# One table set for logarithm and exponential in a two-block transformer kernel

## The chip, the cores and the metric

The kernel runs on one core of a Trainium2 chip. The metric is device time in microseconds (us) of one execution; the time before is the median of three runs. Below, PE is TensorE (matrix products), DVE is VectorE, ACT is ScalarE, POOL is GpSimd and SP is SyncE, which issues nearly all DMAs.

## The reference

An input of 512 tokens by 1024 features passes through a first block of two layers and a second block of two layers, in float32.

```
first block, per layer:
  h = rmsnorm(x, g_pre_mix);  z = h @ w_in
  mLSTM mixer (silu, log_sigmoid gates, exp) and sliding-window attention (softmax)
  x = x + rmsnorm(y @ w_out, g_post_mix)
  h = rmsnorm(x, g_pre_ffn)
  u = causal_dwconv(h @ w_up);  y = (silu(gate) * val) @ w_down
  x = x + rmsnorm(y, g_post_ffn)
second block, per layer, on 512 tokens and (layer 0) 256 context tokens:
  h = rmsnorm(x) modulated by silu(c) @ w_mod;  z = h @ w_in
  pooling, neighborhood attention (softmax), retention (exp decays, silu gate)
  x = x + mod * (y @ w_out);  x = x + mod * conv_ffn(modulated rmsnorm(x))
out = rmsnorm(x, final_g)
```

Every rmsnorm needs x * (mean(x*x) + eps)^(-1/2). The kernel computes the factor on ACT as exp(-0.5 * ln(mean + eps)).

## The kernel before, in words

Features lie on the 128 partitions, tokens on the free axis. A matrix product is done tile by tile (128 output features): each float32 operand is split into a high and a low part, and PE adds three products, high*high, low*high and high*low (`pe_chunk`, line 1011). Per tile, the weights are loaded by SP into `STAGE`, ACT copies them rounded into `WH` (`split_high`, line 850), DVE subtracts to get `WL` (`split_low`, line 856). The same is done with the activations, `HH` and `HL`. The ring of weight buffers has six slots, but four in the third and the fourth of the five streams named below.

The program is a chain of five streams of such products with a mixer (attention and recurrence) between each two. In a stream, every change from one product to the next passes through a *head*, which has its instructions written out in a fixed order on each engine:

- The squares of the last product's output are summed, PE forms their mean (lines 331 and 334), and then runs 24 filler products whose result nobody reads (`idle`, line 257).
- `Rstd.act` (lines 378 to 382) runs on ACT: Ln of the mean (line 380), then, after its own semaphore, Exp (line 382).
- DVE waits for the factor. In `GainHead` it scales y (line 597), adds it to x (line 660), ACT writes the high part (line 638) and a square (line 352), DVE the low part (line 647). In `NormHead` DVE scales x (line 727), ACT writes the high part (line 707), DVE the low part (line 738). PE waits for the low part of each of the eight chunks and multiplies the first three tiles chunk by chunk.
- A `GainHead` has a second `Rstd`, called late: PE is already multiplying unscaled rows, and the factor is multiplied in where DVE takes a tile out of PSUM (line 970, or `to_z1`).
- The one `NormHead` with a gain runs a first `Rstd`, then squares x again on ACT (line 701) with PE summing (line 749), 24 more fillers, then a second `Rstd`.
- `MixHead` (446 to 449) and `RetentionHead` (509 to 531) follow the mixers and have a Ln and an Exp of their own.

ACT can evaluate a function only if the table set loaded in it holds that function. `preload_act_table_set(name)` puts a load of a named set into the program; where a function is not in the current set, the build puts one in, and the profile shows it as ACT_TABLE_LOAD at the line of the instruction that needs it. So line 382 has an ACT_TABLE_LOAD ahead of its Exp although the code asks for none.

Of the kernel before, what the change touches and what calls it, by code (L numbers as in the profile page):

```python
# [46 lines left out]
V2_LP = V2_CB + 44  # L47
V2_N = V2_LP + 6


C_ID, C_BLK, C_RR = 0, 128, 256
C_KE = 384
# [9 lines left out]
def ranges(tokens):  # L62

    return [(0, SEQ)] + ([(SEQ, CTX)] if tokens == TOK else [])
# [17 lines left out]
def by_bank(ap, tokens):  # L82

    return ap if tokens == SEQ else ap.rearrange("p (b s) -> p b s", b=2)
# [20 lines left out]
def later(n):  # L105

    return not isinstance(n, int) or n > 0
# [6 lines left out]
def build(nc, a, out):  # L114
    ctx = ExitStack()
    with ctx:
# [4 lines left out]
        def sb(name, shape, dt=F32, offset=None):  # L121
            size = 4 * int(np.prod(shape[1:]))
            if offset is None:
                offset = used[0]
                used[0] += (size + 31) // 32 * 32
            return nc.alloc_sbuf_tensor_at(name, shape, dt, offset=offset)
# [28 lines left out]
        U = [sb(f"U{s}", [P, SEQ], offset=o_tmp + (2 + 2 * s) * TOK * 4) for s in range(2)]  # L155
# [152 lines left out]
        class Squares:  # L308
# [6 lines left out]
            def act(self, act, c, src, tokens):  # L315
                if c > 1:
                    act.wait_ge(sq_added.sem, sq_added.at(self.added + max(1, c - 2)))
                act.activation(SQ[c % 2][:, 0:tokens], src, ACT.Square).then_inc(sq_done.sem, 1)  # L318
# [174 lines left out]
        class RetentionHead(Head):  # L493
# [13 lines left out]
            def act(self, act):  # L507
                n = self.tokens
                act.activation(Z[:, RG:RG + 3, 0:n], Z[:, RG:RG + 3, 0:n], ACT.Silu).then_inc(gate_done.sem, 1)  # L509
                act.preload_act_table_set("natural_log")  # L510
                self.copied(act, 0)
                self.copied(act, 1)
                self.run.split_high(act, 0)
                for c in range(3):
                    act.wait_ge(centred.sem, centred.at(c + 1))
                    act.activation(GROUP[c][:, 0:n], Z[:, RQ + c, 0:n], ACT.Square).then_inc(group_sq.sem, 1)
                for c in range(2, 5):
                    self.copied(act, c)
                self.run.split_high(act, 1)
                for c in range(3):  # L520
                    act.wait_ge(var_ps.sem, var_ps.at(c + 1))
                    act.activation(GROUP[c][:, 0:n], PS[VAR_PS[c]][:, 0:n], ACT.Ln,
                                   bias=EPSC[:, 0:1]).then_inc(group_ln.sem, 1)
                self.run.split_high(act, 2)
                for c in range(3):
                    act.wait_ge(group_ln.sem, group_ln.at(c + 1))
                    act.activation(GROUP[c][:, 0:n], GROUP[c][:, 0:n], ACT.Exp, scale=-0.5).then_inc(group_rstd.sem, 1)  # L527
                for c in range(5, DC):
                    act.wait_ge(group_out.sem, group_out.at(2 * (c - 4)))
                    self.copied(act, c)  # L530
                for u in range(3, self.run.ring):
                    self.run.split_high(act, u)
# [67 lines left out]
        class GainHead(Head):  # L600
# [21 lines left out]
            def act(self, act):  # L622
                if self.gain:
                    self.before.wait_mean(act)
                    self.first.act(act)
                    act.preload_act_table_set("natural_log")
                else:
                    act.preload_act_table_set("natural_log")
                    act.wait_ge(vec_in.sem, vec_in.at(16))
                    act.wait_ge(filled.sem, filled.at(5))  # L630
                for c in range(DC):
                    if self.gain:
                        act.wait_ge(added.sem, added.at(self.y0 + c + 1))
                    else:
                        if c in self.SPLIT_AT:
                            self.run.split_high(act, self.SPLIT_AT[c])
                        act.wait_ge(x_in[c].sem, x_in[c].at(16))
                    act.activation(self.hi[:, c, :], X[:, c, 0:SEQ], ACT.Identity, scale=self.scale(c),
                                   bias=ZERO[:, 0:1]).then_inc(h_hi.sem, 1)
                    self.squares.act(act, c)  # L640
                if not self.gain:
                    for u in range(4, self.run.ring):
                        self.run.split_high(act, u)
# [29 lines left out]
        class NormHead(Head):  # L673
# [16 lines left out]
            def act(self, act):  # L690
                n = self.tokens
                self.before.wait_mean(act)
                if self.gain:
                    self.first.act(act)
                    act.preload_act_table_set("natural_log")
                    act.wait_ge(ctx_in.sem, ctx_in.at(16))
                    for c in range(DC):
                        act.wait_ge(added.sem, added.at(self.y0 + c + 1))
                        if c > 1:
                            act.wait_ge(xsq_summed.sem, xsq_summed.at(self.x0 + c - 1))  # L700
                        act.activation(SQ[c % 2][:, 0:n], X[:, c, 0:n], ACT.Square).then_inc(xsq_done.sem, 1)
                    act.wait_ge(xsq_summed.sem, xsq_summed.at(self.x0 + DC))
                self.norm.act(act)
                for c in range(DC):
                    act.wait_ge(t_done.sem, t_done.at(self.t0 + c + 1))
                    for st, (t0, tn) in enumerate(ranges(n)):
                        ins = act.activation(self.hi[:, c, t0:t0 + tn], T1[c % 2][:, t0:t0 + tn],
                                             ACT.Identity, bias=self.shift(c, st))
                    ins.then_inc(h_hi.sem, 1)
# [66 lines left out]
        class Run:  # L776
# [149 lines left out]
            def act_out(self, act, tile):  # L926
                seg, t = tile.seg, tile.t
                n = seg.tokens
                if seg.kind == "hidden":
                    s, p = t % 2, tile.hid // 2  # L930
                    buf = (CG, CV)[s]
                    if later(p):
                        act.wait_ge(g_lo.sem, g_lo.at(p))
                    if seg.late:
                        act.wait_ge(acc_free.sem, acc_free.at(tile.n + 1))
                        src = U[s][:, 0:n]
                    else:
                        self.wait_acc(act, tile)
                        src = self.whole(tile)
                    col = t + seg.half * seg.n  # L940
                    bias = seg.vec[:, seg.bias_col + col:seg.bias_col + col + 1] if seg.bias_col is not None else ZERO[:, 0:1]
                    act.activation(by_bank(buf[:, 0:n], n), src, ACT.Identity, scale=tap(seg, t, seg.own),  # L942
                                   bias=bias).then_inc(own_done.sem, 1)
                    if s == 1:
                        if seg.late:
                            act.wait_ge(filtered.sem, filtered.at(tile.flt))
                        else:
                            act.wait_ge(acc_free.sem, acc_free.at(tile.n))
                        act.activation(CG[:, 0:n], CG[:, 0:n], ACT.Silu).then_inc(silu_done.sem, 1)
                        act.wait_ge(gated.sem, gated.at(p + 1))  # L950
                        act.activation(seg.gh[:, t // 2, 0:n], CV[:, 0:n], ACT.Copy).then_inc(g_hi.sem, 1)  # L951
                else:
                    if seg.squares and t == 0:
                        act.preload_act_table_set("natural_log")
                    if seg.out_act:
                        self.wait_acc(act, tile)
                        seg.out_act(act, t, self.whole(tile)).then_inc(acc_free.sem, 1)
                    if seg.squares:
                        act.wait_ge(acc_free.sem, acc_free.at(tile.n + 1))
                        seg.sums.act(act, t, seg.squares(t), n)  # L960
# [238 lines left out]
        class MixPrep:  # L1199
# [24 lines left out]
            def act(self, act, run, tile):  # L1224
# [19 lines left out]
                    act.wait_ge(acc_free.sem, acc_free.at(tile.n - 1))  # L1244
                    act.activation(Z1[:, O1 + t - 10, :], Z1[:, O1 + t - 10, :], ACT.Sigmoid)
                if t == 14:
                    act.preload_act_table_set("exp_and_others")

            def dve(self, dve, run, tile):
                VEC, t = self.vec, tile.t  # L1250
# [32 lines left out]
        def mix1(VEC, ahead):  # L1283
# [20 lines left out]
            U = 4 * NB  # L1304
# [22 lines left out]
            with block() as b:  # L1327
# [131 lines left out]
                def _(act):  # L1459
# [45 lines left out]
                    for s in steps:  # L1505
                        a = s - LAG
# [16 lines left out]
                        if U - 3 <= s < U:  # L1523
                            c = s - U + 3
                            act.wait_ge(o_done.sem, o_done.at(NB * (c + 1)))
                            ahead.first_head.copied(act, c)
                        if a + 1 == U - 1:
                            act.preload_act_table_set("natural_log")

                @b.gpsimd  # L1530
                def _(pool):
# [989 lines left out]
```

## Time and profile before

| what | value |
|---|---|
| runs | 2928.62, 2932.60, 2936.35 us; median 2932.6 |
| profiled execution, its own time | 2934.65 us |
| its span, first to last instruction | 2932.9 us |
| PE busy | 2856.3 us (97%) |
| DVE busy | 1763.2 us (60%) |
| ACT busy | 1160.9 us (40%), 1709 instructions |
| POOL busy | 150.0 us (5%) |
| mean granted TensorE clock | 0.995 |

Busy time of PE includes the fillers. A row of a timeline gives the start in us from the start of the span, the duration, engine, line and operation, output<-input, and in brackets how long the engine sat idle before it and what ended that. Ends of matmuls are modelled and overlap, so a product of 128x512 is shown as 0.39 us although one starts every 0.23 us.

### The profile page before, as it was taken

The page shows a single profiled execution, that of the slowest core. Times are in us where ns is not written, and L with a number is a line of the kernel's source. Part 1 is how long each engine was busy: PE and PEld are TensorE (multiplying, and loading weights), DVE is VectorE, ACT ScalarE, POOL GpSimd, SP SyncE. Part 2 cuts the span into 40 slices and gives each one's busy share as a digit, 9 for nine tenths or more (in the row PEclk, how much of TensorE's full clock was granted, in tenths as well). Part 3 has the DMA queues.
Part 4 walks back from the last instruction along what each step waited for, and adds up shares of the span by engine and source line. Part 5 has one row for each costly group of instructions (what it writes and reads, how often), then busy time and mean ns, then how long its engine had stood idle before and what let it go on. Part 6 is the DMA issues. An engine that isn't in the chain of part 4 may idle for free. (4 is left out here: it accounts for less than half of the span.)

```text
span 2932.9 us, 35827 instructions
## 1 busy us (share of the span) xinstructions
PE 2856.3 (97%) x14618; PEld 2408.2 (82%) x14618; DVE 1763.2 (60%) x2639; ACT 1160.9 (40%) x1709; POOL 150.0 (5%) x172
## 2 busy tenths in 40 slices
PE   9999999999999999999988999999999999999999
PEld 7657888878467888889965999999999975788887
DVE  6667866768567767667665565435534137564563
ACT  5255524443345424342255343213323236543342
POOL 0101000010110000000020100000000002100001
PEclk9999999999999999999999999999999999999999
DMA  5303243343112243326620111121122220232322
GB/s 204 108 15 108 93 134 105 93 130 122 44 59 86 90 147 100 116 85 232 212 66 30 58 58 65 57 73 65 58 58 65 65 97 23 101 101 84 111 83 83
DMA packets 84180, 269.95 MB, mean 92 GB/s; under 512 B 9264, under 2 KB 12208, under 8 KB 83632
## 3 DMA queue, kind: packets, MB, share of 16 engines
q1 hardware_dynamic: 84016, 267.66, 27.9%
q8 instruction: 116, 1.90, 0.3%
q14 instruction: 48, 0.39, 0.0%
HBM read 265.52 MB, written 2.10 MB: 91 GB/s over the span
## 5 line engine op out<-in xcount | busy, mean ns | idle before, releaser
L1011 PE MATMUL PS<-HH,WH 128*128 128x512 f32 (+1 forms) x3032 | 997.9, 366 | 23.7 <-DVE WL L856 8.1
L1011 PE MATMUL PS<-HH,WL 128*128 128x512 f32 (+1 forms) x3032 | 992.9, 364 | 0.0
L1011 PE MATMUL PS<-HL,WH 128*128 128x512 f32 (+1 forms) x3032 | 992.5, 364 | 0.0
L856 DVE TENSOR_TENSOR WL<-STAGE,WH 128x1024 fp32r<-128x1024 f32 (+2 forms) x420 | 482.7, 1151 | 497.5 <-ACT WH L850 497.2
L850 ACT ACTIVATE WH<-STAGE 128x1024 fp32r<-128x1024 f32 (+2 forms) x420 | 407.3, 973 | 621.5 <-DMA STAGE<-in_w_down 274.0
L1011 PEld LDWEIGHTS PS<-HH,WH 128*128 128x128 f32 x3032 | 559.5, 188 | 95.1 <-issue 11.9
L1011 PEld LDWEIGHTS PS<-HL,WH 128*128 128x128 f32 x3032 | 559.9, 188 | 65.4 <-issue 1.9
L1011 PEld LDWEIGHTS PS<-HH,WL 128*128 128x128 f32 x3032 | 559.7, 188 | 64.7
L1011 PE MATMUL PS<-GH,WL 128*128 128x512 f32 (+1 forms) x880 | 294.7, 367 | 0.0
L1011 PE MATMUL PS<-GL,WH 128*128 128x512 f32 (+1 forms) x880 | 294.7, 367 | 0.0
L1011 PE MATMUL PS<-GH,WH 128*128 128x512 f32 (+1 forms) x880 | 294.6, 367 | 0.0
L1011 PEld LDWEIGHTS PS<-GL,WH 128*128 128x128 f32 x880 | 162.7, 188 | 20.6
L1011 PEld LDWEIGHTS PS<-GH,WL 128*128 128x128 f32 x880 | 162.6, 188 | 20.6
L1011 PEld LDWEIGHTS PS<-GH,WH 128*128 128x128 f32 x880 | 162.6, 188 | 20.5
L984 DVE SCALAR_TENSOR_TENSOR CV<-PS,VEC,CV 128x384 f32<-128x384 f32 (+2 forms) x176 | 88.6, 546 | 95.9 <-ACT CV L942 94.4
L951 ACT ACTIVATE GH<-CV 128x512 fp32r<-128x512 f32 (+1 forms) x88 | 60.4, 686 | 190.6 <-DVE CV L993 190.6
L274 DVE SCALAR_TENSOR_TENSOR PS<-MODBUF,X 128x1024 f32<-128x1024 f32 x96 | 126.3, 1315 | 4.4
L984 DVE SCALAR_TENSOR_TENSOR CG<-PS,VEC,CG 128x384 f32<-128x384 f32 (+2 forms) x176 | 88.6, 546 | 56.4 <-ACT CG L942 54.8
L274 DVE SCALAR_TENSOR_TENSOR PS<-MODBUF,COND 128x1024 f32<-128x1024 f32 x64 | 78.9, 1233 | 56.2 <-DMA MODBUF<-in_w_mod 40.6
L970 DVE TENSOR_TENSOR U<-PS,RSTD 128x512 f32<-128x512 f32 x88 | 60.7, 690 | 85.2 <-PE PS L1011 73.7
L995 DVE TENSOR_TENSOR GL<-CV,GH 128x512 fp32r<-128x512 f32 (+1 forms) x88 | 66.8, 759 | 66.2 <-ACT GH L951 66.2
L325 POOL TENSOR_TENSOR SQSUM<-SQ,SQ 128x512 f32<-128x512 f32 (+1 forms) x8 | 12.4, 1555 | 1702.8 <-ACT SQ L318 1702.8
(233 smaller groups left out, 2544.9 us busy)
## 6 DMA issues: line engine op xcount, KB each, us to landing
STAGE<-in_w_up SPq DMA_DIRECT2D x176, 512.0 KB, 3.3
MODBUF<-in_w_mod SPq DMA_DIRECT2D x96, 512.0 KB, 4.2
STAGE<-in_w_in SPq DMA_DIRECT2D x84, 512.0 KB, 3.4
STAGE<-in_w_down SPq DMA_DIRECT2D x64, 384.0 KB, 3.1
STAGE<-in_w_down SPq DMA_DIRECT2D x64, 320.0 KB, 2.9
STAGE<-in_w_out SPq DMA_DIRECT2D x32, 512.0 KB, 4.7
BM<-in_na_bias SPq DMA_DIRECT2D x24, 256.0 KB, 2.6
CR<-in_const_ret SPq DMA_DIRECT2D x2, 1152.0 KB, 5.2
```

Of the source, the lines that this page charges most:

```text
L274: dve.scalar_tensor_tensor(out=PS[2][:].rearrange("p (c j) -> p c j", c=DC), in0=MODBUF[2 * self.l + buf][:], scalar=1.0, in1=cond, op0=AL ...
L325: pool.tensor_tensor(SQSUM[:, 0:tokens], SQ[0][:, 0:tokens] if c == 1 else SQSUM[:, 0:tokens], SQ[c % 2][:, 0:tokens], ALU.add).then_inc(s ...
L850: act.activation(WH[unit.slot][:, 0:size], STAGE[unit.slot][:, 0:size], ACT.Copy).then_inc(w_hi.sem, 1)
L856: dve.tensor_tensor(WL[unit.slot][:, 0:size], STAGE[unit.slot][:, 0:size], WH[unit.slot][:, 0:size].bitcast(F32), ALU.subtract).then_inc(w ...
L951: act.activation(seg.gh[:, t // 2, 0:n], CV[:, 0:n], ACT.Copy).then_inc(g_hi.sem, 1)
L970: dve.tensor_tensor(U[s][:, 0:n], self.whole(tile), RSTD[:, 0:n], ALU.mult).then_inc(acc_free.sem, 1)
L984: ins = dve.scalar_tensor_tensor(out=buf[:, a0 + shift:a0 + shift + an], in0=src[:, a0:a0 + an] if seg.late else self.acc(tile, col, an), ...
L995: dve.tensor_tensor(seg.gl[:, t // 2, 0:n], CV[:, 0:n], seg.gh[:, t // 2, 0:n].bitcast(F32), ALU.subtract).then_inc(g_lo.sem, 1)
L1011: ins = pe.matmul(self.acc(tile, col, tn), w[:, c:c + P], r[:, k, t0:t0 + tn], start=(k == 0 and m == 0), stop=(k == seg.kc - 1 and m == 2))
```

## The change

Seven preloads stand in the code before. Four are kept and now name the set `natural_log_exp_and_others`, which holds both Ln and Exp: lines 510, 628 and 954, which had named `natural_log`, and line 1247, which had named `exp_and_others`. Three are deleted: lines 626, 695 and 1528.

```
+LOG_EXP = "natural_log_exp_and_others"
...
             def act(self, act):
                 n = self.tokens
                 act.activation(Z[:, RG:RG + 3, 0:n], Z[:, RG:RG + 3, 0:n], ACT.Silu).then_inc(gate_done.sem, 1)
-                act.preload_act_table_set("natural_log")
+                act.preload_act_table_set(LOG_EXP)
...
                 if self.gain:
                     self.before.wait_mean(act)
                     self.first.act(act)
-                    act.preload_act_table_set("natural_log")
                 else:
-                    act.preload_act_table_set("natural_log")
+                    act.preload_act_table_set(LOG_EXP)
                     act.wait_ge(vec_in.sem, vec_in.at(16))
...
                 if self.gain:
                     self.first.act(act)
-                    act.preload_act_table_set("natural_log")
                     act.wait_ge(ctx_in.sem, ctx_in.at(16))
...
                     if seg.squares and t == 0:
-                        act.preload_act_table_set("natural_log")
+                        act.preload_act_table_set(LOG_EXP)
...
                 if t == 14:
-                    act.preload_act_table_set("exp_and_others")
+                    act.preload_act_table_set(LOG_EXP)
...
                             ahead.first_head.copied(act, c)
-                        if a + 1 == U - 1:
-                            act.preload_act_table_set("natural_log")
```

## Rows read from the trace of the kernel before

**Rows 1.** The page, part 1: busy time, share, instructions.
```profile
PE 2856.3 (97%) x14618; PEld 2408.2 (82%) x14618; DVE 1763.2 (60%) x2639; ACT 1160.9 (40%) x1709; POOL 150.0 (5%) x172
```

**Rows 2.** Groups by line, ACT: table loads; busy us, mean ns, idle before.
```profile
L382 ACT ACT_TABLE_LOAD x13 | 16.7, 1283 | 0.2
L954 ACT ACT_TABLE_LOAD x8 | 10.3, 1283 | 0.1
L626 ACT ACT_TABLE_LOAD x3 | 3.8, 1283 | 0.1
L1240 ACT ACT_TABLE_LOAD x2 | 2.6, 1283 | 0.0
L1528 ACT ACT_TABLE_LOAD x2 | 2.6, 1283 | 0.0
L449 ACT ACT_TABLE_LOAD x2 | 2.6, 1283 | 0.0
L527 ACT ACT_TABLE_LOAD x2 | 2.6, 1283 | 0.0
L695 ACT ACT_TABLE_LOAD x1 | 1.3, 1283 | 0.0
```

**Rows 3.** Timeline, ACT, the head at 259 us.
```profile
259.19 0.69 ACT L380 ACTIVATE RSTD<-PS,EPSC 128x512 f32<-128x512 f32 x1 [0.27 <-PE PS L334]
259.90 1.28 ACT L382 ACT_TABLE_LOAD   x1
261.19 0.63 ACT L382 ACTIVATE RSTD<-RSTD 128x512 f32<-128x512 f32 x1
261.84 1.28 ACT L626 ACT_TABLE_LOAD   x1
263.91 0.81 ACT L638 ACTIVATE HH<-X,ZERO,VEC 128x512 fp32r<-128x512 f32 x1 [0.78 <-DVE X L660]
```

**Rows 4.** Timeline, PE: fillers, and the first product after them.
```profile
258.99 5.52 PE L257 MATMUL PS<-MEAN 128*128 128x128 f32 x48
265.85 0.50 PE L1011 MATMUL PS<-HH,WH 128*128 128x512 f32 x1 [1.34 <-DVE HL L647]
...
1283.88 0.62 PE L1011 MATMUL PS<-HH,WH 128*128 128x384 f32 x2 [1.31 <-DVE HL L738]
```

**Rows 5.** Timeline: DVE at 632 us; PE at 1267 us.
```profile
631.93 1.41 DVE L597 SCALAR_TENSOR_TENSOR Y<-Y,VEC,RSTD 128x512 f32<-128x512 f32 x2 [1.10 <-ACT RSTD L382]
...
1266.65 10.56 PE L749 MATMUL PS<-SQ,MEAN 128*128 128x512 f32 x32 [1.00 <-ACT SQ L701]
```

**Rows 6.** Timeline, DVE and PE, a late Rstd at 914 us.
```profile
917.22 1.23 DVE L856 TENSOR_TENSOR WL<-STAGE,WH 128x1024 fp32r<-128x1024 f32 x1 [0.25 <-ACT WH L850]
...
918.59 0.47 PE L1011 MATMUL PS<-HH,WH 128*128 128x512 f32 x1 [2.29 <-DVE WL L856]
```

**Rows 7.** Windows: stretch, its length, busy PE, PEld, DVE, ACT, POOL; clock, DMA, GB/s.
```profile
117.77:209.32 91.55, 81.56 (x424) 41.11 (x425) 58.19 (x137) 48.10 (x122) 11.90 (x29) 0.98 0.06 24
743.40:836.86 93.46, 84.34 (x425) 42.13 (x425) 58.29 (x137) 48.11 (x122) 11.90 (x29) 0.95 0.06 23
...
918.90:922.20 3.30, 3.30 (x9) 2.56 (x8) 3.26 (x5) 1.65 (x2) 0.00 (x0) 0.51 0.03 12
```

**Rows 8.** Timeline, PE, the second RetentionHead and the head after it.
```profile
2518.79 0.50 PE L1011 MATMUL PS<-HH,WH 128*128 128x512 f32 x1 [0.79 <-DVE HL L537]
...
2560.20 0.48 PE L1011 MATMUL PS<-HH,WH 128*128 128x512 f32 x1
```

**Rows 9.** The chain of waits at the end: start us, us, what.
```profile
2922.91 1.28 ACT L382
```

**Rows 10.** Timeline: ACT and PE around the first MixHead.
```profile
206.58 0.60 ACT L1487 ACTIVATE PTT<-PS 128x512 f32<-128x512 f32 x1 [0.52 <-PE PS L1383]
211.62 0.63 ACT L449 ACTIVATE XF<-XF 128x512 f32<-128x512 f32 x1
...
215.56 1.88 PE L486 MATMUL PS<-XF,CST 128*128 128x512 f32 x4
```

More of the change, by code:

```diff
@@ L48 @@
 V2_N = V2_LP + 6
+LOG_EXP = "natural_log_exp_and_others"
 C_ID, C_BLK, C_RR = 0, 128, 256
@@ L509, in act @@
                 act.activation(Z[:, RG:RG + 3, 0:n], Z[:, RG:RG + 3, 0:n], ACT.Silu).then_inc(gate_done.sem, 1)
-                act.preload_act_table_set("natural_log")
+                act.preload_act_table_set(LOG_EXP)
                 self.copied(act, 0)
@@ L625, in act @@
                     self.first.act(act)
-                    act.preload_act_table_set("natural_log")
                 else:
-                    act.preload_act_table_set("natural_log")
+                    act.preload_act_table_set(LOG_EXP)
                     act.wait_ge(vec_in.sem, vec_in.at(16))
@@ L694, in act @@
                     self.first.act(act)
-                    act.preload_act_table_set("natural_log")
                     act.wait_ge(ctx_in.sem, ctx_in.at(16))
@@ L953, in act_out @@
                     if seg.squares and t == 0:
-                        act.preload_act_table_set("natural_log")
+                        act.preload_act_table_set(LOG_EXP)
                     if seg.out_act:
@@ L1246, in act @@
                 if t == 14:
-                    act.preload_act_table_set("exp_and_others")
+                    act.preload_act_table_set(LOG_EXP)
             def dve(self, dve, run, tile):
@@ L1526, in _ @@
                             ahead.first_head.copied(act, c)
-                        if a + 1 == U - 1:
-                            act.preload_act_table_set("natural_log")
                 @b.gpsimd
```

## The prediction

> **What bounds the kernel now.** The page's first part says PE is busy 97% of the span and ACT 40% [rows 1]. So ScalarE time as such is worth nothing: whatever leaves ACT counts only where PE stands still for it. Some of the 97% is filler, too, in the heads, where PE has nothing of its own to do. I therefore read three things: the groups by line, for which table loads exist; the timeline of PE, for every idle gap; and the timelines of ACT and DVE back from each gap, for whether a removed load lies in the chain that ended it. The windows give the clock, and the chain of waits gives the end of the program.
>
> In a typical head [rows 3] Ln takes 0.69 us, a table load of 1.28 stands behind it, then comes Exp, and then another load (line 626). PE meanwhile runs its 24 fillers, which end at 258.99 + 5.52 = 264.51, and still idles 1.34 until the first low part [rows 4]. That is the bound to look for: the head's chain is later than the fillers, by a little more than one load.
>
> **What the change removes.** It goes by which set is current when each function comes. With one set for Ln and Exp, the load in front of Exp goes wherever the named set was loaded before Ln: 13 at line 382, 2 at 449, 2 at 527. The three deleted preloads take 3 (626), 1 (695) and 2 (1528) with them. That is 23 loads of 1.283 us, 29.5 us of ACT [rows 2]. What stays is what follows Silu or Sigmoid. The pair at lines 1240 and 1242 stays as well: it comes after Silu with no preload, and the build fetches a set for Exp and then another for Ln, as it did before. At line 954 eight preloads stay; the four that follow a mixer's head now name a set that is already loaded. Whether they still appear as instructions I can't see. They precede a wait for DVE, so I cost them at nothing either way, between 0 and 4 x 1.28 if that cover were gone.
>
> **What of it lies on the path.** Each place is costed by the smallest of three: the load (1.28), PE's gap, and the time that DVE sat waiting for the factor.
>
> - The heads at 266 and 893 us (two GainHeads with the same gap): the load at 382 is in the chain, and the gap of 1.34 is larger than the load [rows 3, 4]. 2 x 1.28 = 2.56. PE will then idle 0.06 behind its fillers, so fillers are late next. The load at 626 is hidden: the high part behind it waited another 0.78 for DVE [rows 3], and both ends move together. Worth 0.
> - The head at 636 us: DVE was splitting weights and waited only 1.10 for the factor [rows 5]. 1.10; DVE's split is late next.
> - The NormHead with a gain: PE waits 1.00 after its first fillers for the first square [rows 5]. Its products over eight chunks of 768 columns then run on without a stop, so their start counts: 1.00, and the fillers are late next. The load at 695 is hidden, as at 626. Behind the second Rstd the gap is 1.31 [rows 4]: 1.28 more, since everything ahead moved too. Together 2.28.
> - The two other heads of 768 tokens (1682 and 2243 us) repeat the pattern of the one at 1284, whose gap is 1.31 [rows 4]: 2 x 1.28 = 2.56.
> - The head at 2560 us: no idle in front of its first product [rows 8]. 512 tokens without a gain is a short chain; the fillers cover it. 0.
> - The second RetentionHead: the load at 527 precedes its Exps, and PE waits 0.79 for the low part that follows from them [rows 8]. 0.79, then PE's own work is late next. In the first one, with 768 tokens, PE has half as much again to do and no such gap. 0.
> - MixHead (449, twice): Exp ends at 212.25 and PE asks for it at 215.56 without having idled [rows 10]. 0. Line 1528, twice: the copy behind it still waited 0.52 for PE [rows 10]. 0.
> - Late Rstds, four: three have no PE gap behind them. 0. The one at 914 us lies in a run with four weight slots. Behind the Exp stand a weight split on ACT and, on DVE, the take-out of the first tile and then the low part of the weights, for which PE waits 2.29 [rows 6]. 1.28 goes. Here the clock matters too: just behind that gap the granted clock is 0.51 for 3.3 us, about the lower level of 1.2 GHz, after PE had stood still 2.29 us, and 9 products stand in it [rows 7]. By the clock it lost 0.49 x 3.3 = 1.6; by its products, which start 0.23 us apart at full clock, 3.3 - 9 x 0.23 = 1.2. I take 1.5, between the two, and expect a gap of 1.0 to keep the full clock, as the gaps of 1.3 in rows 4 do. Its bounds are 0 and 1.6.
> - The last Rstd: its load is in the chain that ended last [rows 9], with only DVE's scaling and the store behind it. 1.28.
>
> Sum: 2.56 + 1.10 + 2.28 + 2.56 + 0.79 + 1.28 + 1.28 = 11.85, and 1.5 of clock: 13.4 us. From the profiled execution's own time, 2934.65 - 13.4 = 2921.3. The median of the runs before is 2.05 lower, 2932.6, and so the forecast for the median is 2919.2, a ratio of 0.9954.
>
> On the price of one load, the trace gives 1.28 and nothing around it: Ln ends at 259.88, the load runs from 259.90, Exp starts at 261.19 [rows 3]. The Trainium skill, "ScalarE: Activation LUTs", section "What ACT_TABLE_LOAD costs", adds a drain of about 1.38 us and puts a switch at about 2.66 us. In this chain Exp waits for Ln in any case, and the trace shows no such second part.
>
> **The rivals.**
>
> A, the forecast: 13.4 us, 2919.2. Own range 2915.5 to 2923.
>
> B, a switch costs more than its row shows, say twice 1.28. Then the gaps are the cap, not the load: 1.34 x 2, 1.10, 1.00, 1.31 x 3, 0.79, 2.29, and 2.56 at the end, 14.4, and 1.5 of clock: 15.9, or 2916.7. For it: nothing in the rows. Against it: rows 3 leave 0.02 us on either side of the load. The page's 2.66 would come out the same within 0.1.
>
> C, part of it is given back. The drop of clock at 918 remains (1.5), and in the heads of the four-slot run (1284, 1682 and 2243 us, 3.8 us) the next weights become the late thing, since their transfers are asked for when PE frees a slot. 13.4 - 5.3 = 8.1, or 2924.5. For it: rows 6 show that with four slots PE does run into its weights. Against it: slots are freed by PE, so those transfers move with the head.
>
> D, the change doesn't do what it says: the build puts a load in front of Exp anyway, or had chosen sets well before. No difference, 2932.6. Against it: sets named by the code are kept as named, and 13 loads at 382 stand at an Exp that follows a set without it [rows 2]. The Trainium skill, "ScalarE activation tables: per-element evaluation and per-set limits", section "Table sets in the compiler and the runtime", says that the back end places loads by the longest run that one set serves. By that rule Ln and Exp would share a set already, and the change would give nothing; rows 2 disagree with it here.
>
> E, slower: the clock. PE has a new rhythm everywhere behind 266 us, and the mixers are thin enough in products to sit at the edge. The two first-block mixers are the same program, and the second takes 93.46 us against 91.55, at a granted clock of 0.95 against 0.98 [rows 7]: 1.9 us for the price of a worse draw. A drop in a dense stretch costs 1.5 [rows 7]. It decides from nine new drops in the streams (13.5 us, against 13.4 saved), or seven with two mixers drawn worse (7 x 1.5 + 2 x 1.9 = 14.3, or 2933.5). With fifteen it would be 2919.2 + 22.5 = 2941.7. Against it: gaps only get shorter.
>
> **How the numbers follow.** A 0.68, B 0.06, C 0.17, D 0.06, E 0.03. A measurement of this kernel can tell about 0.3% from no change, 8.8 us. A and B are beyond it. C lies at the bound, so I put 0.08 of it on faster and 0.09 on no change. Of E, 0.02 is beyond the bound. Faster 0.82, same 0.06 + 0.09 + 0.01 = 0.16, slower 0.02. The likeliest is A, 2919.2. The range goes from 2914.5, which is B less 2.2 for the scatter of a median (single runs lie 4.0 below and 3.8 above it), up to 2926, which is C and 1.5; it leaves out D, E and the edges of C and B, some 0.15.
>
> **What would show it.** In the changed profile: no table load at 382, 449, 527, 626, 695 and 1528; Exp about 0.02 us behind the end of Ln; gaps behind the fillers below 0.1 us where they were 1.3; about 0.8 at 636; about 1.0 in place of 2.29 at the late Rstd near 914, and a full clock behind it; the last factor 1.28 earlier relative to the last product. It is wrong if those gaps stay at 1.3, if new waits for weights appear behind the heads, or if stretches of half clock multiply.

## The result and the profile after

The changed kernel takes 2917.45 us (median of 5 runs, 2915.08 to 2921.14); the kernel before, beside it, takes 2932.6 (median of 5, 2928.62 to 2936.35). The ratio is 0.9949, 95% interval 0.9934 to 0.9964: 15.2 us faster, where 13.4 were forecast. The profiled execution's own time is 2915.08 us, its span 2913.4, its mean granted clock 0.998; before they were 2934.65, 2932.9 and 0.995. A second pair, both kernels run again, gave 2933.71 and 2917.82.

The page's first part, against [rows 1]:

```profile
PE 2848.2 (98%) x14618; PEld 2405.3 (83%) x14618; DVE 1762.5 (60%) x2639; ACT 1130.7 (39%) x1686; POOL 149.8 (5%) x172
```

ACT has 23 instructions and 30.2 us less; 23 loads of 1.283 are 29.5. The number of matmuls is the same. The groups by line for ACT, table loads only, show what stayed (columns as in [rows 2]; 27 loads in all, against 50):

```profile
L954 ACT ACT_TABLE_LOAD x8 | 10.3, 1283 | 0.1
L949 ACT ACT_TABLE_LOAD x4 | 5.1, 1283 | 0.1
L1240 ACT ACT_TABLE_LOAD x2 | 2.6, 1283 | 0.0
L1242 ACT ACT_TABLE_LOAD x2 | 2.6, 1283 | 0.0
...
L512 ACT ACT_TABLE_LOAD x2 | 2.6, 1283 | 0.0
```

No load is left at the Exp of an Rstd (line 384 now). The four of line 954 that name a set already loaded are still instructions of 1283 ns each, and lines 1240 and 1242 still fetch two sets one after the other.

The same head as in [rows 3], in the timeline of ACT:

```profile
257.46 0.69 ACT L382 ACTIVATE RSTD<-PS,EPSC 128x512 f32<-128x512 f32 x1 [0.27 <-PE PS L336]
258.19 0.63 ACT L384 ACTIVATE RSTD<-RSTD 128x512 f32<-128x512 f32 x1
...
260.90 0.81 ACT L639 ACTIVATE HH<-X,ZERO,VEC 128x512 fp32r<-128x512 f32 x1 [2.08 <-DVE X L661]
```

Exp starts 0.04 us behind the end of Ln, where 1.31 lay between them. At the high part the idle before it grew from 0.78 to 2.08, by 1.30: the load that stood there (line 626) had been hidden under the wait for DVE.

The timeline of PE, against [rows 4, 5, 6, 8] (in brackets the idle before, and what ended it):

```profile
257.26 5.52 PE L259 MATMUL PS<-MEAN 128*128 128x128 f32 x48
262.85 0.50 PE L1011 MATMUL PS<-HH,WH 128*128 128x512 f32 x1
...
631.75 0.50 PE L1011 MATMUL PS<-HH,WH 128*128 128x512 f32 x1 [0.71 <-DVE HL L648]
...
909.85 0.47 PE L1011 MATMUL PS<-HH,WH 128*128 128x512 f32 x1 [1.01 <-DVE WL L856]
...
1255.17 10.54 PE L749 MATMUL PS<-SQ,MEAN 128*128 128x512 f32 x32
1271.09 0.61 PE L1011 MATMUL PS<-HH,WH 128*128 128x384 f32 x2
...
1306.12 0.59 PE L1011 MATMUL PS<-HH,WH 128*128 128x384 f32 x2 [1.45 <-DVE WL L856]
...
2541.92 0.48 PE L1011 MATMUL PS<-HH,WH 128*128 128x512 f32 x1
```

The 1.34 behind the fillers at 266 us has no idle noted in its place now; the first square of the NormHead (1.00) and the head behind it (1.31) the same. The gap at the late Rstd went from 2.29 to 1.01. The wait for weights at 1306 us is 1.45, and the same wait before was 1.33: the only place of this pair where something seems to be given back, 0.13 us.

The chain of waits at the end, against [rows 9] (start, us, what):

```profile
2903.91 0.70 ACT RSTD L382
2904.61 0.02 issue
2904.63 0.64 ACT RSTD L384
2905.27 0.03 issue
2905.30 0.75 DVE X L767
```

**Where 19.57 us of the two profiles went.** The two profiled executions differ by 2934.65 - 2915.08 = 19.57 us. The start of the same instruction in both traces gives a running difference; its steps are the gains. This list of steps is called the ledger below. Steps at loads: 266 us 1.25, 636 us 1.24, 893 us 1.29, 914 us 1.28, 1267 us 1.19, 1284 us 1.29 less the 0.13 given back, 1682 us 1.29, 2243 us 1.33, the second RetentionHead 0.94, the end 1.26. They sum to 12.2 (11.85 forecast). The rest, 7.3, is the clock, as the windows show (columns and the stretches before as in [rows 7]; first after, then two stretches of before that stand in no group):

```profile
117.61:207.59 89.98, 79.99 (x425) 40.66 (x425) 58.18 (x137) 46.81 (x121) 11.85 (x29) 1.00 0.07 24
739.18:830.69 91.51, 81.52 (x424) 41.13 (x425) 58.17 (x137) 46.80 (x121) 11.85 (x29) 0.98 0.07 24
...
909.90:913.20 3.30, 3.30 (x15) 2.72 (x16) 3.27 (x5) 1.59 (x3) 0.00 (x0) 1.00 0.47 159
1584.70:1588.30 3.60, 3.60 (x14) 3.60 (x13) 2.76 (x4) 3.49 (x5) 0.00 (x0) 0.53 0.00 0
2404.00:2407.50 3.50, 3.50 (x11) 1.71 (x9) 3.43 (x8) 1.97 (x4) 0.00 (x1) 0.52 0.02 5
```

```profile
1492.30:1495.70 3.40, 3.37 (x10) 1.98 (x11) 3.33 (x8) 2.30 (x4) 0.00 (x0) 0.52 0.03 5
2502.70:2506.10 3.40, 3.40 (x10) 2.68 (x9) 3.05 (x5) 2.26 (x4) 0.00 (x0) 0.51 0.33 133
```

The mixers gave 1.57 and 1.95, the stretch behind the late Rstd 1.57, those at 1492 and 2503 us 1.66 and 1.47, and one at 1585 us that only the changed kernel's profile has took 1.06 back. That is 7.2, with 0.16 at the opening 7.3. So what the loads don't explain is short stretches of half clock (1.2 GHz), in part at different places in the two executions. Whether it belongs to the change, one profile of each kernel can't say. That was the first question for the runs.

### The profile page after: what moved, and what is told of

Read it like the earlier page. It is cut to its first block and busy times, and to the rows that moved or that the text cites. A ratio compares the mean times of both kernels' runs of the same rounds, so it can differ in the third digit from the quotient of the medians.

```text
span 2913.4 us, 35804 instructions
## 1 busy us (share of the span) xinstructions
PE 2848.2 (98%) x14618; PEld 2405.3 (83%) x14618; DVE 1762.5 (60%) x2639; ACT 1130.7 (39%) x1686; POOL 149.8 (5%) x172
## 5 line engine op out<-in xcount | busy, mean ns | idle before, releaser
L327 POOL TENSOR_TENSOR SQSUM<-SQ,SQ 128x512 f32<-128x512 f32 (+1 forms) x8 | 12.4, 1555 | 1695.5 <-ACT SQ L320 1695.5
```

What stands on the lines that cost most here:

```text
L327: pool.tensor_tensor(SQSUM[:, 0:tokens], SQ[0][:, 0:tokens] if c == 1 else SQSUM[:, 0:tokens], SQ[c % 2][:, 0:tokens], ALU.add).then_inc(s ...
```

## The experiments

**Both kernels once more.** No edit; the ledger of a second pair of executions, and where their clock falls.

> The kernel before once more, unchanged. Theory 1: which short stretches of half clock an execution has is a draw of that execution and not a property of the kernel. Then this profile has another set of such stretches than the first one (which had them near 144, 765, 919, 1492, 2421 and 2503 us), each worth 1.5 to 2 us, while every gap behind the fillers is the same to 0.1 us (1.34, 1.91, 1.34, 1.00, 1.31, 1.31, 1.44). Median 2930 to 2935. Rival: the stretches are fixed by what the kernel does (the gap of 2.29 us above all), and the same ones come back, so that the 7 us by which the two spans differ beyond the loads belong to the change.

> The changed kernel once more, unchanged. Theory 1: the stretches of half clock differ from those of its first profile (near 765, 1585 and 2404 us); the gaps are the same to 0.1 us (none behind the fillers at 264, 887, 1256, 1273 and 1667 us, 0.7 at 632, 0.16 at 2228, 1.01 at 910). Median 2915 to 2920. Rival: the same three stretches come back, and the changed kernel really has fewer of them.

Measured: 2933.71 us (ratio to the kernel before beside it 1.0001, 0.9992 to 1.001) and 2917.82 (0.9943, 0.9931 to 0.9956). Spans of the profiled executions: 2928.5 and 2916.1, 12.4 apart. With the same steps at the loads, 12.2, this pair leaves 0.2 for the clock, where the first left 7.3. The wait for weights near 1306 us is 1.48 in both kernels this time, so the 0.13 given back in the first pair is scatter. The late Rstd in the timeline of PE, and the windows of the kernel before run again:

```profile
918.98 0.47 PE L1011 MATMUL PS<-HH,WH 128*128 128x512 f32 x1 [2.29 <-DVE WL L856]
```

```profile
915.00:922.00 7.00, 4.71 (x21) 3.62 (x20) 5.05 (x7) 5.28 (x7) 0.00 (x0) 1.00 0.22 79
142.40:149.20 6.80, 5.27 (x12) 1.70 (x12) 3.31 (x10) 2.50 (x8) 0.29 (x1) 0.53 0.01 2
1586.20:1589.60 3.40, 2.33 (x4) 1.23 (x5) 0.00 (x0) 3.07 (x4) 0.00 (x0) 0.57 0.40 108
```

The same kernel, the same gap of 2.29, and a clock of 1.00 behind it. So the drop of [rows 7] doesn't follow from the gap, and my 1.5 us had the wrong reason. Its mixer instead has 6.8 us of half clock at 142 us.

The theory that each execution draws its own places held only in part. The kernel before had half clock near 144, 765, 919, 1492, 2421 and 2503 us; run again it has it near 143, 767 and 2498 once more, not at the three others, and newly near 1587. In the changed kernel the theory missed: its three places (765, 1585 and 2404 us) all came back (769, 1588 and 2407), with one more near 141. So most places recur, and some come and go.

**The loads of the heads put back.** 13 loads stood at line 382; this returns the nine of the heads and leaves the four late ones out.

```
-            def act(self, act):
+            def act(self, act, late=False):
...
                 act.wait_ge(log_done.sem, log_done.at(self.n + 1))
+                if not late:
+                    act.preload_act_table_set(LOG_EXP)
                 act.activation(RSTD[:, 0:n], RSTD[:, 0:n], ACT.Exp, scale=-0.5).then_inc(rstd_done.sem, 1)
...
-                            head.late.act(act)
+                            head.late.act(act, late=True)
```

> The changed kernel with one load put back between Ln and Exp in the nine Rstds that are not late. Theory (a load costs its 1.28 us where the gap or DVE's wait lets it through): 1.28 at 264, 887, 1273, 1667, 2228 us and at the end, 1.10 at 632, 1.00 at 1257, 0 at 2542: 9.8 us more than the changed kernel, 2927.2. Rival (a switch of sets costs about double, and a load of the set that is already there is cheap): under 5 us more, or 18 and more. Rival (only the sum of ACT's busy time counts): 9 x 1.28 = 11.5 more.

Measured: 2930.32 us (0.9985, 0.9977 to 0.9994), 12.5 above the changed kernel beside it. PE's timeline has the gaps of the kernel before again, 1.34, 1.00 and 1.31 to the hundredth:

```profile
266.14 0.50 PE L1013 MATMUL PS<-HH,WH 128*128 128x512 f32 x1 [1.34 <-DVE HL L650]
636.24 0.50 PE L1013 MATMUL PS<-HH,WH 128*128 128x512 f32 x1 [1.91 <-DVE HL L650]
1264.07 10.56 PE L751 MATMUL PS<-SQ,MEAN 128*128 128x512 f32 x32 [1.00 <-ACT SQ L703]
1281.30 0.62 PE L1013 MATMUL PS<-HH,WH 128*128 128x384 f32 x2 [1.31 <-DVE HL L740]
2239.28 0.61 PE L1013 MATMUL PS<-HH,WH 128*128 128x384 f32 x2 [1.44 <-DVE HL L740]
```

The ledger of its profile returns 10.1 us at the heads and the end (9.8 expected). The other 2.4 of the medians fit the clock: its 11 runs have a mean of 0.9957, those of the changed kernel beside it 0.9968, and over the 21 runs of the kernel before beside it the time moves by 2.2 us for 0.001 of mean clock. One load in front of an Exp of a head is thus worth its 1.2 to 1.3 us, with no other edit. The load put back names the set that is already current, and it costs what the load removed cost, which had changed the set: 1283 ns in the row, and the same step on the path.

**The covered loads put back.** Eight loads return where I had costed them at nothing: behind the first Rstd's Exp (the old lines 626 and 695), in the mixer (1528), and in the MixHead in front of Exp (449).

```
                 act.wait_ge(head_ln.sem, head_ln.at(1))
+                act.preload_act_table_set(LOG_EXP)
                 act.activation(MEAN2, MEAN2, ACT.Exp, scale=-0.5).then_inc(head_rstd.sem, 1)
...
                     self.first.act(act)
+                    act.preload_act_table_set(LOG_EXP)
...
                             ahead.first_head.copied(act, c)
+                        if a + 1 == U - 1:
+                            act.preload_act_table_set(LOG_EXP)
```

> The changed kernel with eight loads put back where the prediction called them covered: behind the first Exp of the four heads with a gain, late in the first-block mixers (twice), and between Ln and Exp of MixHead (twice). Theory: nothing, 0 +- 0.5 us in every stretch of the profile, median 2915 to 2920. Rival (each load costs, wherever it stands): 8 x 1.28 = 10.3 us more, 2927.7.

Measured: 2918.89 us (0.9948, 0.9935 to 0.996), 1.1 above the changed kernel beside it, within the scatter of both. In the ledger of its profile no head moves by more than 0.04 us, and from the end of a mixer to behind its MixHead it moves by at most 0.03. So 10.3 us of ScalarE cost PE nothing that can be measured.

**The late loads put back.** Four loads, of which only the one at 914 us was costed.

```
+                if late:
+                    act.preload_act_table_set(LOG_EXP)
                 act.activation(RSTD[:, 0:n], RSTD[:, 0:n], ACT.Exp, scale=-0.5).then_inc(rstd_done.sem, 1)
```

> The changed kernel with one load put back between Ln and Exp in the four late Rstds. Theory: three of them are covered (31, 283 and 652 us: 0), and the one at 907 us lies ahead of the weights for which PE waits: the gap there goes from 1.01 to 2.29, 1.28 us, and the longer gap lets the clock fall behind it in part of the executions (up to 1.5 more). Median 1.3 to 2.8 above the changed kernel, 2919 to 2920.6. Rival: late loads are all covered, 0.

Measured: 2920.46 us (0.9955, 0.9942 to 0.9967). PE's timeline:

```profile
915.70 0.47 PE L1013 MATMUL PS<-HH,WH 128*128 128x512 f32 x1 [2.30 <-DVE WL L858]
```

The gap is back, the ledger returns 1.26 at this place, and the three others return nothing. The granted clock behind it is 1.00 again, and so it is in the kernel before with 30 fillers (below), which has the gap of 2.29 too: three executions in which this gap brings no drop, against one. The median is 2.6 to 3.0 us above the changed kernel's; what goes beyond 1.26 is within the scatter.

**More fillers, with the change and without.** If the fillers are what is late in the heads now, six more cost their own time in the changed kernel and little in the one before.

```
-                    idle(pe, 24, 3)
+                    idle(pe, 30, 3)
```

> The changed kernel with 30 fillers behind each mean in place of 24 (1.38 us more PE work each). Theory (with the loads gone the fillers are what PE is late for): 1.32 at 263 and 886, 0.67 at 632, 1.38 and 1.35 in the head of two Rstds at 1255 and 1271, 1.35 at 1668, 1.22 at 2228, 1.38 at 2542, 0 at the end: 10.0 us more, 2927.5. Rival (the chain on ACT and DVE is still late, fillers are free): under 3 us.

> The kernel before with 30 fillers in place of 24. Theory: the gaps of 1.31 to 1.91 behind the fillers swallow them: 0.04 at 266 and 893, 0 at 636 and 2243, 0.38 and 0.07 at 1267 and 1284, 0.07 at 1682, and 1.38 at 2560 where no gap was: 2.0 us more than the kernel before at the same clock, and perhaps less if the clock falls more seldom with the gaps filled. Rival (fillers cost the same in both kernels): 10 us more.

Measured: 2925.2 us (0.9973, 0.9963 to 0.9982), 7 to 8 above the changed kernel; and 2934.9 (1.0004, 0.9995 to 1.0013), 1.4 above the kernel before, of which its trace shows 1.32 at the head of 2560 us, where fillers covered the chain already [rows 8]. The theories had put them at 10.0 and 2.0. The timeline of PE with the change and 30 fillers (60 products a place):

```profile
257.97 6.86 PE L259 MATMUL PS<-MEAN 128*128 128x128 f32 x60
264.58 0.48 PE L1011 MATMUL PS<-HH,WH 128*128 128x512 f32 x1
...
1254.90 6.86 PE L259 MATMUL PS<-MEAN 128*128 128x128 f32 x60
1261.60 0.59 PE L749 MATMUL PS<-SQ,MEAN 128*128 128x512 f32 x1
```

Six fillers are 6.86 - 5.52 = 1.34 us of records. The ledger returns 1.32 at 2542 us and 1.28 at 1256, where only fillers hold PE, about 1.0 at 263, 886, 1271, 1668 and 2228, and 0.40 at 632, where 0.71 of idle was left: some 8 us in all. So in the changed kernel the fillers end together with the chain, or up to 0.3 ahead of it: at the five heads of 1.0 the chain is still the later one by that much. Where they hold PE, as here, the first product starts before the record of the last filler ends: 257.97 + 6.86 = 264.83 against 264.58, 0.25 earlier. In the changed kernel it started at 262.85, 0.07 behind 262.78. That is 0.3 of waiting for which no bracket stands: the ends of matmuls are modelled, idle is counted from them, and a bracket behind fillers is some 0.3 too short.

**Fewer fillers.** `idle(pe, 18, 3)` in both places.

> The changed kernel with 18 fillers in place of 24. Theory: the chain is only 0.0 to 0.1 us behind the fillers, so it becomes the bound at once: nothing at most heads, 0.3 less at 1255, 1.3 less at 2542 (where the low part is ready 1.4 us before PE takes it): 1.6 us less at the same clock, 2916.2. Rival (the clock): gaps of 1.4 behind the fillers let it fall more often, as in the kernel before, which gives back 2 us or more: 2918 to 2920.

Measured: 2918.14 us (0.9946, 0.9933 to 0.9958), no gain. PE's timeline, and the window behind the second of these gaps:

```profile
263.83 0.50 PE L1011 MATMUL PS<-HH,WH 128*128 128x512 f32 x1 [1.40 <-DVE HL L648]
632.71 0.50 PE L1011 MATMUL PS<-HH,WH 128*128 128x512 f32 x1 [2.05 <-DVE HL L648]
```

```profile
633.80:637.20 3.40, 3.40 (x10) 2.63 (x9) 3.40 (x7) 2.65 (x4) 0.00 (x0) 0.52 0.00 0
```

The chain holds PE as before, so only the head at 2542 us gains, 1.31. The gap at 632 grew from 0.71 to 2.05, and behind it the clock is 0.52 for 3.4 us, which cost 1.6. The mean clock of its runs is 0.9952, nearly that of the kernel before beside it (0.9951), where the changed kernel has 0.9968. This fits the rival, that the clock takes back what fewer fillers give. It is not shown: the 1.6 us at stake are less than the interval can tell, and that the gap of 2.05 brought the drop rests on one profile. The Trainium skill, "TensorE: Matmul & The Clock Gate", Part 1 ("The HAM clock gate"), describes a clock that falls when the engine is not kept busy; this trace agrees at 632 us, but the three late Rstds with 2.29 and 2.30 of idle and a clock of 1.00 show that a gap of this size alone doesn't decide it.

**Silu behind the first copies of the RetentionHead.** PE waits about 2 us for weights there, behind Silu and a preload on ACT; the copies and the split were moved ahead of them.

```
-                act.activation(Z[:, RG:RG + 3, 0:n], Z[:, RG:RG + 3, 0:n], ACT.Silu).then_inc(gate_done.sem, 1)
-                act.preload_act_table_set(LOG_EXP)
...
                 self.run.split_high(act, 0)
+                for c in range(2, 5):
+                    self.copied(act, c)
+                act.activation(Z[:, RG:RG + 3, 0:n], Z[:, RG:RG + 3, 0:n], ACT.Silu).then_inc(gate_done.sem, 1)
+                act.preload_act_table_set(LOG_EXP)
```

> The changed kernel with another order on ScalarE at the start of both heads after the second-block mixers: five copies and the first weight split stand ahead of Silu and its two table loads (4.7 and 4.0 us), not behind them. Theory (a table load hurts only where it stands ahead of what PE waits for): the first weights' low part is ready 1.3 us earlier at 1583 us and 2.0 at 2485, of which the squares, now later, leave 1.3: 2.6 us less, and the gaps of 1.83 and 2.06 in front of the products fall to 0.55 and near 0, so that the half clock seen behind 1585 us (1.1 us) is rarer: 2914 to 2915.5. Rival (the squares behind Silu become late and hold the variance products): no gain or slower.

Measured: 2917.8 us (0.9947, 0.9933 to 0.996), no gain. ACT's timeline, then PE's in this run; last, PE's in the changed kernel and in the kernel before run again:

```profile
1585.76 1.06 ACT L850 ACTIVATE WH<-STAGE 128x1024 fp32r<-128x1024 f32 x1 [2.11 <-DMA STAGE<-in_w_out]
```

```profile
1582.10 5.80 PE L573 MATMUL PS<-Z,CS 128*128 128x512 f32 x12 [2.57 <-PEq L1826]
...
1591.05 0.59 PE L1011 MATMUL PS<-HH,WH 128*128 128x384 f32 x2 [0.47 <-DVE WL L856]
...
2490.34 0.47 PE L1011 MATMUL PS<-HH,WH 128*128 128x512 f32 x1 [0.72 <-DVE WL L856]
2495.29 1.98 PE L581 MATMUL PS<-SQ,CS 128*128 128x512 f32 x4 [1.29 <-ACT SQ L520]
```

```profile
1575.63 4.11 PE L573 MATMUL PS<-Z,CS 128*128 128x512 f32 x12 [2.57 <-PEq L1826]
```

```profile
1595.91 0.58 PE L1011 MATMUL PS<-HH,WH 128*128 128x384 f32 x2 [0.47 <-DVE WL L856]
```

In the second place (2485 us) the gap for weights shrinks from 2.06 to 0.72, but the squares come later, PE waits 1.29 for them, and the ledger ends 0.2 us behind the changed kernel. There the theory that Silu was the price fell: the squares are late next. The first place can't tell. The split waits 2.11 us for its DMA and still starts 2.5 us earlier than before (3.66 behind the first product of line 573, where it was 6.17). But the 12 products of that line ran at half clock (5.80 us against 4.11), DVE waited for them, and the first product of the weights came 8.95 us behind their start, where it was 8.61. The small gap of 0.47 there is a reading to beware of: the kernel before run again, which has no such edit, shows the same 0.47 behind products at half clock.

**Six loads and one row of fillers out.** The four redundant loads of line 954 and the doubled one in front of line 1240 go; the head at 2542 us, the only one covered by its fillers alone, gets 18.

```
-                    if seg.squares and t == 0:
+                    if seg.squares and t == 0 and seg.weights is not a["w_out"] and seg.weights is not a["w_out2"]:
...
-                            idle(pe, 24, 3)
+                            idle(pe, 18 if seg.weights is a["w_out2"] and seg.tokens == SEQ else 24, 3)
...
                 if t == 8:
+                    act.preload_act_table_set(LOG_EXP)
                     act.wait_ge(gate_in.sem, gate_in.at(1))
```

> The changed kernel with what the profile after shows to be idle work: 18 in place of 24 fillers in the one head where the fillers hid the whole chain (2542 us), the four loads of a set that is already there left out, and one load in place of two in front of the logarithm of the gates (twice). Theory: 1.3 us from the fillers, 0 from the six loads, which are covered: 2916.5. Rival (fillers there keep the clock up): no gain. Rival (loads cost wherever they stand): 6 x 1.28 + 1.3 = 9 us less.

Measured: 2918.07 us (0.9947, 0.9935 to 0.996). The profile has 21 table loads in place of 27. The ledger shows 1.33 less at 2542 and nothing at the loads; a single 1.33 doesn't show in the medians.

**Fillers in the mixer.** Every profile without these fillers, of either kernel and of all the edits, has half clock near 142 or 767 us, around a wait of PE in the mixer. Six fillers go into it.

```
                     def summed(m):
                         h, i = divmod(m, NB)
+                        if m == NB:
+                            pe.wait_ge(num_kept.sem, num_kept.at(1))
+                            idle(pe, 6, 3)
                         pe.wait_ge(p_done.sem, p_done.at(m + 1))
```

> The changed kernel with six fillers (1.28 us) in the gap of 1.66 us in both first-block mixers (143 and 765 us), behind which nearly every profile so far shows the granted clock at 0.5 for 3.4 to 10.2 us. Theory (the idle gap is what lets the clock fall): the half clock there goes or shortens; each 3.4 us of it costs 1.5 to 1.9, so 1.5 to 4 us less than the changed kernel. Rival (the clock falls for what stands ahead of the gap, the thin products of the whole stretch): no change, or up to 2.6 us more where the fillers themselves run at half clock.

Measured: 2916.05 us (0.9943, 0.993 to 0.9955). PE's timeline in the changed kernel, the same place with fillers, and the windows there:

```profile
142.94 1.13 PE L1417 MATMUL PS<-PT,VT 128*128 128x512 f32 x2 [1.66 <-DVE PT L1602]
```

```profile
141.06 1.60 PE L259 MATMUL PS<-MEAN 128*128 128x128 f32 x12
142.80 1.13 PE L1420 MATMUL PS<-PT,VT 128*128 128x512 f32 x2
```

```profile
142.00:149.00 7.00, 6.22 (x28) 2.64 (x27) 4.80 (x11) 3.75 (x10) 0.72 (x3) 1.00 0.00 0
765.00:775.00 10.00, 9.35 (x46) 3.80 (x44) 5.59 (x15) 5.74 (x17) 0.85 (x4) 1.00 0.00 0
```

The stretches of half clock in the mixers are gone; only one, near 2401 us, is left. The mean clocks of its five runs are 0.997 to 0.999. The median moved by less than the interval can tell.

**Both of the last two.**

> The changed kernel with the edits of trimmed and mixfill together, as the version to keep. Theory: 1.3 us from the six fillers that are gone at 2542 us (trimmed's profile showed 1.33 there) and about 1.7 from the clock in the two first-block mixers, where six fillers kept it at full speed: 2914.6, some 3 us under the changed kernel, and no stretch of half clock near 143 and 765 us. Rival (mixfill's profile was a lucky draw): half clock at 143 or 765 us comes back, and the median is that of trimmed, 2918.

Measured: 2913.07 us (2911.76 to 2917.43; 0.9937, 0.9924 to 0.9951), 4.4 us below the changed kernel by their medians (2914.6 was forecast), 1.8 to 3.5 by their ratios (0.9943 and 0.9949 for the changed kernel). It is the fastest version here, though the intervals overlap. Half clock stands near 1480 and 1576 us in its profile, and in neither first-block mixer:

```profile
117.00:210.00 93.00, 83.43 (x444) 43.50 (x444) 59.56 (x139) 48.32 (x123) 11.86 (x29) 1.00 0.08 29
739.00:832.00 93.00, 83.70 (x446) 43.92 (x447) 59.31 (x139) 48.33 (x123) 11.85 (x29) 1.00 0.07 25
```

## Why the prediction was right, and where it wasn't

The direction and the size were right: 13.4 us forecast, 15.2 and 15.9 measured by the medians of two pairs. The mechanism is the one named, with three sizes a little off and one reason wrong. The loads account for 12.2 of what was measured; that the sum with 1.5 of clock came so near the total is in part luck.

- **Which loads go.** All 23, as forecast, and the pair at 1240 and 1242 stayed. The four redundant ones of line 954 stayed as instructions; leaving them out gave nothing. D fell.
- **Loads in the chain of a head.** Ten places (nine at Rstds, one in the second RetentionHead) were costed at 11.85 with the end; 12.2 measured. The terms capped by a gap were too small: 1.00 measured 1.19, 1.10 measured 1.24, 0.79 measured 0.94. Two of the caps were brackets behind PE's modelled ends; the run with 30 fillers shows such a bracket to be up to 0.3 short. The third was DVE's; that it is short for a like reason is argued only. Where the load itself was the smaller, 1.28 measured 1.25 to 1.33. One reading was off without harm: the gap at 2243 us was 1.44, not the 1.31 of the head at 1284, and 0.16 of it is left.
- **Covered loads.** Costed at zero. Eight of them put back cost nothing visible, nor did three late ones.
- **What is late next.** The fillers, nearly as forecast: six more cost 7 to 8 us with the change and 1.4 without. But only at 1256 us do they alone hold PE anew; at five heads the chain is still some 0.3 later, for which no idle is noted. At 636 us the split of DVE is late (0.71 of idle is left), also as forecast.
- **C**, given back by the weights: 0.13 us at one place in the first pair and nothing in the second, where it had 3.8. That the slots move with the head fits this.
- **B**, a switch dearer than its row: fell at the end of the program, where nothing caps it. The last load, put at 1.28, gave 1.26. The Trainium skill, "ScalarE: Activation LUTs", section "What ACT_TABLE_LOAD costs", gives about 2.66 us for a switch; by it the end would have given about 2.66 us. The trace does not agree, in a chain where Exp depends on Ln.
- **The clock.** This step failed in its reason. I put 1.5 us on one drop at 918 us and tied it to the gap of 2.29. Three other executions (the kernel before run again and with 30 fillers, and the late loads put back) have that gap and no drop. What the runs show is a clock a little higher over all: mean 0.995 over the runs of the kernel before, 0.997 over those of the changed one, and medians that beat the 12.2 of the loads by 3 to 4 us. Within the changed kernel's five runs the time follows the clock (2915.08 us at 0.998, 2921.14 at 0.995). The 0.0019 between the means (0.9949 and 0.9968 for the second pair), at 2.2 us for 0.001, would be 4.2 us, an estimate that covers the 3 to 4. With the nine loads of the heads back the mean is 0.9957, so part of the higher clock seems to go with them. Half clock near 2500 us stands in all three profiles of kernels with all their loads, and in none of those with the change, but it is worth 1.5 of the 3 to 4. Where the rest sits, and why the clock is higher, stays open, since a run without a profile gives only its mean.
- **E**, a worse clock from a new rhythm, didn't come: nine new drops were needed; in the first pair one appeared, at 1585 us, and four went (144, 919, 1492 and 2503 us), and the place at 1585 is not the change's own, for the kernel before run again has it too.

## What to carry to other kernels

Price a removed table load by the smallest of its own row, the idle that the bottleneck engine shows behind it and the wait of the engines between, and not by ScalarE's busy time: of 23 loads ten paid, 0.94 to 1.33 us each. An idle counted behind matmuls can be a few tenths short. Ask at once what is late next, here fillers sized for the longer chain; taking them down gave nothing at these heads, since the chain is still as late. Before a stretch of half clock is tied to a cause, profile the same kernel a second time and see whether it stays there; and before a gap is said to have shrunk, look whether the work ahead of it ran at half clock.

## What the runs showed of the hardware

A preload of a set that is already current is not dropped, and it takes as long as one that changes the set: 1283 ns each, at four preloads of line 954 in the changed kernel and at all 21 loads put back in the three runs that do so. In front of an Exp on the path it moves what follows by 1.2 to 1.3 us, as did the loads of another set that were removed at the same places.

Half clock comes and goes between executions of one program, at places of which most recur. Outside the mixers the kernel before had it at 919, 1492, 2421 and 2503 us in one profile, at 1587 and 2498 in another, and the two spans differ by 4.4 us. Over all fourteen profiles it stands between 1576 and 1593 us in eleven and between 2401 and 2421 us in nine, but at 919 and at 634 us in one each. Twelve small products in a wait of 1.66 us in the mixer kept the clock at 1.00 through both mixers in two of two profiles; the twelve others show half clock in one or both.
